# The up product of a feed-forward layer by seven half-size products of block sums, in two passes

## What is computed

```python
h = rmsnorm(x, g_ffn[i])
u = jnp.einsum("bsd,df->bsf", h, w_up[i])            # w_up: 1024 x 5632
f_gate = causal_dwconv(u[..., :D_FF], conv_f_w[i]) + conv_f_b[i]   # D_FF = 2816, 3 taps
f = jax.nn.gelu(f_gate, approximate=True) * u[..., D_FF:]
x = x + jnp.einsum("bsf,fd->bsd", f, w_down[i])      # w_down: 2816 x 1024
```

## Time and profile before

| | us |
|---|---|
| median of 3 runs | 2114.32 |
| lowest, highest | 2111.88, 2114.84 |
| profiled execution, time | 2106.84 |
| profiled execution, span | 2105.1 |
| PE busy in the span | 2044.3 |

### The profile page before, as it was taken

One profiled execution on the slowest core, in us unless ns is written; L12 is line 12 of the kernel. 1 busy time (PEld: TensorE's weight loads), 2 busy tenths in 40 slices (PEclk: granted clock), 3 DMA queues, 4 the chain that ended last, 5 costly groups with the idle time before them and its releaser, 6 DMA issues.

```text
span 2105.1 us, 24958 instructions
## 1 busy us (share of the span) xinstructions
PE 2044.3 (97%) x9797; PEld 1696.9 (81%) x9797; DVE 1177.0 (56%) x1119; ACT 439.1 (21%) x547; POOL 730.4 (35%) x534
## 2 busy tenths in 40 slices
PE   6999999999999999999999999999999999999998
PEld 5888788888887888888888888888788878888887
DVE  4999995312546755665565655745443745556520
ACT  4000001302222000000000000243222235555411
POOL 2444355444323343333333343423122511112221
PEclk9999999999999999999999999999999999999999
DMA  4211111241122122211222112211113210000033
GB/s 135 60 41 50 40 45 45 65 115 50 48 84 79 40 71 80 60 59 43 76 70 70 50 50 80 73 32 36 40 60 110 76 41 1 11 11 1 1 131 90
DMA packets 176852, 122.08 MB, mean 58 GB/s; under 512 B 8772, under 2 KB 160273, under 8 KB 176785
## 3 DMA queue, kind: packets, MB, share of 16 engines
q1 hardware_dynamic: 175504, 118.77, 18.7%
q10 hardware_dynamic: 1280, 2.35, 0.3%
HBM read 112.71 MB, written 8.39 MB: 58 GB/s over the span
## 4 chain that ended last, share of the span: by engine, by line
PE 79%; DVE 7%; issue 4%; POOL 4%; DMA 4%; ACT 3%; SPq 0%; POOLq 0%; DVEq 0%; ACTq 0%
PE ps L488 67%; POOL wlo L437 2%; DMA raw<-in_w_up 2%; PE ps L882 2%; POOL whi L435 1%; DVE prob L1878 1%; PE ps L896 1%; PE ps L893 1%; PE ps L899 1%; PE ps L915 1%; PE ps L890 1%; PE ps L917 1%; PE ps L916 1%; PE ps L902 1%; PE ps L705 1%
## 5 line engine op out<-in xcount | busy, mean ns | idle before, releaser
L437 POOL TENSOR_TENSOR wlo<-raw,whi 128x1024 fp32r<-128x1024 f32 (+2 forms) x162 | 459.1, 2834 | 13.5
L434 POOL TENSOR_TENSOR small<-ones 128x1 f32<-128x1 f32 x166 | 50.4, 304 | 1109.8 <-PE ps L488 916.3
L488 PE MATMUL ps<-xb_hi,whi 128*128 128x512 f32 x1216 | 378.6, 393 | 10.2 <-POOL wlo L437 3.5
L488 PE MATMUL ps<-xa_hi,whi 128*128 128x512 f32 x1184 | 372.5, 394 | 2.6 <-POOL wlo L437 1.1
L488 PE MATMUL ps<-xb_lo,whi 128*128 128x512 f32 x1216 | 375.0, 390 | 0.0
L488 PE MATMUL ps<-xb_hi,wlo 128*128 128x512 f32 x1216 | 374.5, 389 | 0.0
L488 PE MATMUL ps<-xa_lo,whi 128*128 128x512 f32 x1184 | 368.0, 390 | 0.0
L488 PE MATMUL ps<-xa_hi,wlo 128*128 128x512 f32 x1184 | 367.6, 389 | 0.0
L488 PEld LDWEIGHTS ps<-xb_hi,whi 128*128 128x128 f32 x1216 | 226.0, 188 | 64.1 <-POOL wlo L437 7.5
L488 PEld LDWEIGHTS ps<-xb_hi,wlo 128*128 128x128 f32 x1216 | 228.3, 188 | 48.1
L488 PEld LDWEIGHTS ps<-xb_lo,whi 128*128 128x128 f32 x1216 | 228.3, 188 | 48.1
(11 more groups left out here) (325 smaller groups left out, 2245.6 us busy)
## 6 DMA issues: line engine op xcount, KB each, us to landing
raw<-in_w_in SPq DMA_DIRECT2D x52, 512.0 KB, 3.8
raw<-in_w_up SPq DMA_DIRECT2D x44, 512.0 KB, 4.2
raw<-in_w_down SPq DMA_DIRECT2D x22, 512.0 KB, 3.5
w_mod<-in_w_mod SPq DMA_DIRECT2D x40, 256.0 KB, 2.9
x_columns<-in_x SPq DMA_DIRECT2D x8, 512.0 KB, 4.8
raw<-in_w_o SPq DMA_DIRECT2D x8, 512.0 KB, 3.8
raw<-in_w_ple_gate SPq DMA_DIRECT2D x8, 512.0 KB, 3.7
y_scratch<-resid SPq DMA_DIRECT2D x8, 512.0 KB, 3.1
```

The costliest lines, as they stand in the source:

```text
L434: nc.gpsimd.tensor_tensor(small[:, 106 + slab.slot:107 + slab.slot], ones[:, 0:1], ones[:, 0:1], ALU.mult)
L437: nc.gpsimd.tensor_tensor(lo, src, f32(hi), ALU.subtract).then_inc(split_done, 1)
L488: ins = mm(dst[j], w, r[j], start=first and f, stop=last and l)
```

## The change

The up product and the down product become two passes.

**Up pass.** The first two tiles (gate and up) are done as before, in four jobs. For each of the other 20 tiles the two weight tiles (gate, up) and the two halves of the 1024 input features form a 2 x 2 block matrix `A`, and the two halves of the features by the two halves of the tokens a 2 x 2 block matrix `B`. The product of the two is made from 7 products of blocks instead of 8 (Strassen's scheme in Winograd's form): four sums of weight blocks (`weight_sums`, on DVE, S1 to S4) and four sums of input blocks (`token_comb`, once, 128 x 2048 each), seven products (`combination`, 12 matmuls of 512 columns, each into its own PSUM bank), and seven additions that read PSUM (`comb_pair`). ACT makes the high part of each weight block (`weight_hi`) into a ring of four halves of `whi`, POOL the low part (`comb_split`). ACT also does the first tap and copies the first product out of PSUM. The input sums are built from `R` times `g_ffn` before the norm's factor is known. The finished f tile goes to a DRAM scratch (`f_store`). On DVE, ACT, POOL and SP the pairs run in hardware loops of two or four; the last four pairs are written out on DVE and ACT.

**Down pass.** Five chunks of four tiles and one of two. The f tiles come back from DRAM (`f_load`), ACT makes their high parts (`f_hi`), POOL the low parts (`f_low`, but for two that DVE makes). A down job has 24 matmuls (12 in the last chunk), a slab serves two jobs. The modulation's rows are now loaded by ACT's queue, four buffers deep, and accumulated behind the down jobs, on average 1.4 rows (two accumulations each) per job (`mod_rows_at`).

```diff
+        def combination(q, u, n):
...
+            if n == 0:
+                pe.wait_ge(sem("st_copied"), q * 4 + (u + 1))
+            else:
+                pe.wait_ge(sem("st_read"), q * 40 + (10 * u + (1, 3, 4, 6, 7, 9)[n - 1]))
+            pe.wait_ge(sem("st_split"), q * 28 + (g + 1))
...
+            for k in range(4):
+                w = slice(cols.start + k * P, cols.start + (k + 1) * P)
+                for i, (wp, bp) in enumerate(((whi, bh), (whi, bl), (wlo, bh))):
+                    last = mm(o, wp[:, s, w], bp[:, k, :], start=k == 0 and i == 0, stop=k == 3 and i == 2)
...
+        def comb_pair(q, u, following):
...
+            kept, summed = T[3][:, first], T[3][:, second]
+            P2 = product(1)
+            dve.wait_ge(sem("st_copied"), q * 4 + (u + 2))
+            step(tt(T[0][:, 2:2 + H], P2, kept, ALU.add))
+            after(1)
+            step(tt(T[0][:, 2:2 + H], T[0][:, 2:2 + H], rbc[:, first], ALU.mult))
+            step(tt(summed, product(2), kept, ALU.add))
+            P7 = product(3)
+            after(3)
+            step(tt(kept, P7, summed, ALU.add))
+            if following is not None:
+                weight_sums(*following)
+            P5 = product(4)
+            after(4)
+            dve.wait_ge(sem("f_ready"), t)
+            step(tt(T[2][:, second], P5, kept, ALU.add))
+            step(tt(summed, P5, summed, ALU.add))
+            P3 = product(5)
+            after(6)
+            step(tt(T[0][:, 2 + H:2 + S], P3, summed, ALU.add))
+            after(7)
+            step(tt(T[0][:, 2 + H:2 + S], T[0][:, 2 + H:2 + S], rbc[:, second], ALU.mult))
+            step(tt(T[2][:, first], product(6), kept, ALU.add))
+            after(9)
+            step(tt(T[2][:, 0:S], T[2][:, 0:S], rbc[:, :], ALU.mult))
+            taps(t)
+            after(10)
+            dve.wait_ge(sem("gelu"), t + 1)
+            tt(T[1][:, 0:S], T[1][:, 0:S], T[2][:, 0:S], ALU.mult).then_inc(sem("f_ready"), 1)
...
+        def comb_out(q, u, final=False):
...
+            fn(T[3][:, 0:H], PS[:, 0:H], ACT.Copy).then_inc(sem("st_copied"), 1)
+            weight_hi(q, g + 4)
+            weight_hi(q, g + 5)
+            gelu(q * 4 + (u + 1))
+            weight_hi(q, g + 6)
+            if not final:
+                for n in range(7, 10):
+                    weight_hi(q, g + n)
...
+            act.wait_ge(sem("st_read"), q * 40 + (10 + 10 * u + 8))
+            act.wait_ge(sem("f_out"), t * 16)
+            fn(T[1][:, 0:S], T[0][:, 0:S], ACT.Identity, scale=dcol("conv_f_w", t), bias=dcol("conv_f_b", t)).then_inc(sem("fc_tap"), 1)
+            if not final:
+                weight_hi(q, g + 10)
...
+        def mod_rows(rs):
...
+                if r >= 4:
+                    act.wait_ge(sem("mod_mac"), 2 * r - 5)
...
+        for c in range(NDC):
+            if 1 <= c:
+                rows_until(c - 1, 3)
+                f_hi(c, range(f_tiles(c)))
...
+                for c in range(NDC):
+                    for k in range(2 if c in (0, NDC - 1) else 4):
+                        split(L + (4 * c + k + (2 if c == 0 else 0)))
+                        if k == 1 and c < NDC - 1:
+                            f_low(c + 1)
```

More of the change, by code:

```diff
@@ L20 @@
 NF = DFF // P
-FC = 2
-NCH = NF // FC
+NDC = 6
+PAIRS = NF - 2
+MODG = 3 * D // H
 PLE = 256
@@ L336, in mod_rows @@
[L336 to L349, removed]
@@ new lines, in tensor_program @@
+        pe.wait_ge(pair_free[0], (Lin(JOBS["ffn"]) + 4).half())
+        with pe.Fori(0, PAIRS // 4) as q:
+            for u in range(4):
+                for n in range(7):
+                    combination(q, u, n)
+        J, L = Lin(JOBS["down0"]), Lin(SLABS["down"])
+        pe.wait_ge(pair_free[0], J.half())
+        pe.wait_ge(pair_free[1], J.half())
+        pe.wait_ge(split_done, L.val(1))
+        hi, lo = f_parts(0)
+        pe.wait_ge(sem("st_copied"), PAIRS + 1)
+        pe.wait_ge(sem("st_read"), 10 * PAIRS + 4)
@@ new lines, in tensor_program @@
+        for k in range(4):
+            if k < 2:
+                pe.wait_ge(sem("f_lo"), k + 1)
+            else:
+                pe.wait_ge(sem("tc_dve"), k + 5)
+            for m in range(2):
+                w = slice(k * 2 * P + m * P, k * 2 * P + m * P + P)
+                last = split_products([pair(J + m, 0, H), pair(J + m, H, S)], whi[:, 0, w], wlo[:, 0, w],
+                                      [hi[:, k, 0:H], hi[:, k, H:S]], [lo[:, k, 0:H], lo[:, k, H:S]], k == 0, k == 3,
+                                      1 if k == 0 and m == 0 else None)
+                if k == 3:
+                    last.then_inc(job_done, 1)
@@ L686, in tensor_program, with columns_due, hook @@
             transposes(Lin(JOBS["p"] + k), [pstage[:, t, k * P:(k + 1) * P] for t in range(8)])
[L687 to L699, removed]
+        def columns_due(c):
+            def hook(m):
+                of = 8 * c + m - 3
+                for g in range(MODG):
+                    if 8 * g + 7 in mod_rows_at(of // 8, of % 8):
+                        pe.wait_ge(sem("mod_read"), g + 1)
+                        mod_columns(g, 16 * (g + 1) + 1)
+            return hook
+        for c in range(1, NDC - 1):
+            ffn_down(c, between=columns_due(c))
         def square_sums(m):
@@ new lines, in vector_program @@
+        first_tap(1)
+        taps(1)
+        first_up(1)
+        dve.wait_ge(job_done, JOBS["ffn"] + 4)
+        weight_sums(0, 0)
+        first_product(1)
+        with dve.Fori(0, PAIRS // 4 - 1) as q:
+            for u in range(4):
+                comb_pair(q, u, (q, u + 1))
+        q = PAIRS // 4 - 1
+        for u in range(4):
+            comb_pair(q, u, (q, u + 1) if u < 3 else None)
+        for k in (2, 3):
+            dve.wait_ge(sem("f_hi"), k + 1)
+            tt(f_parts(0)[1][:, k, :], fraw[FSLOT[0]][:, k, :], f32(f_parts(0)[0][:, k, :]), ALU.subtract).then_inc(sem("tc_dve"), 1)
@@ new lines, in vector_program @@
+        dve.wait_ge(sem("cs"), 2)
+        for c in range(NDC - 1):
+            if c == 1:
+                for k in range(2):
+                    J = Lin(JOBS["p"] + k)
+                    dve.wait_ge(sem("pt_hi"), k + 1)
+                    tt(XAl[:, 4 + k, :], pair(J), f32(XAh[:, 4 + k, :]), ALU.subtract).then_inc(*one(free(J)))
+            for m in range(8):
+                down(c, m)
+                if mod_rows_at(c, m):
+                    for r in mod_rows_at(c, m):
+                        g, k = r // 8, r % 8
+                        if r == 0:
+                            dve.wait_ge(sem("f_out"), 16 * NF)
+                        if k == 4 and g:
+                            read_mod(g - 1)
+                        dve.wait_ge(sem(f"modw_in{r % 4}"), 16 * (r // 4 + 1))
+                        for n in range(2):
+                            mod_mac(k, n, mod_row_buffer(r), 16 * g + 1, g % 2)
```

526 lines of the change are left out of this document (353 added, 173 removed).

## The result

The changed kernel takes 2099.86 us (median of 4 runs, 2099.18 to 2101.82); the kernel before, timed beside it, 2113.1 (4 runs, 2111.12 to 2114.84). The ratio is 0.9939, with a 95% interval of 0.9922 to 0.9956: 0.6% faster, where I had forecast 1.2% slower. 2099.86 is within a microsecond of rival A. The span of the profiled execution is 2097.4 us, 7.7 less than before.

The account below looks back on a forecast made before the run. PE's matmul count was taken as the bound. Terms -54.4 - 8.4 + 44 + 8 + 32 + 5 gave +26: span 2131, median 2140.5 us, 1.2% slower; range 2098 to 2168.

Parts of the forecast that it names:

- rival A: Up loop: subtracts fall beside VectorE's PSUM reads and waits, cycle is PE's 19.04 us; 2100.5 us, chance 0.22.
- Term 1: Up product: twenty tile pairs take 84 matmuls instead of 96, 240 fewer in all; -54.4 us.
- Term 2: Old feed-forward loop: PE's waits for POOL's weight splits, five times 1.7 us, go with that loop; -8.4 us.
- Term 3: Up loop: VectorE's work, gaps and collisions with POOL's subtracts make a 21.8 us cycle per pair; +44 us, bounds 0 and 68.
- the old loop's 38%: Old feed-forward loop: VectorE's taps and accumulations lose 53 us of 140 us of POOL subtracts, at lower VectorE load.
- a layout: Up loop: one pair laid out by hand, VectorE losing 4.6 us, 50% of the 9.1 us of POOL subtracts.
- the point where the sign changed: Up loop: a cycle of 20.5 us, with 3.3 us of blocking instead of 4.6, divides slower from faster.
- Term 4: Before the up loop: the four token sums are covered by the first two tile pairs; cost 0, up to 5 us.
- Term 5: Passage from up to down: late first low parts, VectorE's residual add and the f load delay PE; +8 us, bounds 3 and 15.
- Term 6: Down pass, chunks 1 to 3: queue order delays the third slab's split, PE waits 7.4 + 13.0 + 11.3; +32 us.
- Term 7: Down pass and passage: PE's clock is slow after three long waits and the passage; +5 us, 0 to 12.
- Rival D: Up loop: seven banks in turn with PE waits lower the clock for a third of the loop; 2200 us, chance 0.03.

Follow-up runs that it names:

- the run with two extra sums: Changed kernel with the first weight sum computed two extra times in each up pair on VectorE: 2111.5 us.
- the run with three orders: Changed kernel with GpSimd's next-chunk low parts after the fourth split, VectorE's first weight sums before the taps, and its low parts 2 and 3 before the last product: 2062.3 us.
- two runs: Changed kernel with ScalarE issuing high parts after job 0's w_mod rows, 2065.9 us; or with GpSimd making low parts after the fourth slab's split, 2061.47 us.
- the runs with extra sums: Changed kernel with the first weight sum computed extra times per up pair: one 2103.2 us, two 2111.5, four 2145.8.

## Why the prediction was wrong

The direction was wrong, and one term of the sum decided it: VectorE's cycle in the up loop.

- **Term 1, matmuls, right.** -54.4 us: 1656 matmuls in 378.38 us, a cycle of 19.04.
- **Term 2, the loop's split waits**, -8.4: the split waits of the old loop are gone from the up loop. The trace of before lists only 3.5 us of them (7 waits between 690 and 1340); most of the rest of the 8.4 came from taking 0.2267 us for every matmul, where a stretch of whole jobs has 54.72 / 240 = 0.2280.
- **Term 3, VectorE in the up loop, +44, was 0: the step that failed.** Predicted cycle 21.8 us, own cycle by the runs 18.0. The 3.8 us are two errors. Work and gaps were 17.1 in the sum and are 18.0 - 3.3 = 14.7: I took one tap's idle time of 0.15 us for all 13 dependent steps, and took durations as if they added, where the trace has the next operation start 0.60 or 0.71 us after one of 0.69. That is 2.4 us. The blocking by GpSimd was 4.6 and is 3.3 in the run with two extra sums, 36% of the subtracts and not 50: near the old loop's 38%, which I had and overruled with a layout. That is 1.3. With the first alone mended the cycle would have been 19.4 and the sum about -12; with the second alone 20.5, the point where the sign changed. Both together put VectorE 1.0 us under PE, and the term at its lower bound.
- **Term 4, before the loop**, 0, was 3.3 us of wait and 2.8 of slow matmuls (13 in 5.72 us). The token sums do find cover; what failed is that I priced only them. The sums of the first pair's weights stood behind `taps(1)` and `first_up(1)`; with them ahead of `taps(1)`, in the run with three orders, the wait and the slow matmuls were gone.
- **Term 5, from up to down**, +8: waits of 1.4, 0.3, 4.6 and 0.5, 6.8 us. The size holds. Its second half doesn't: the residual add cost 0.5 and not 2.6 behind the squares of ctx. It became a wait of 4.2 only when the low parts were moved.
- **Term 6, the down pass, right.** 7.75 + 13.02 + 11.80 = 32.6 us against 7.4 + 13.0 + 11.3, by the chain laid out, and two runs took it away.
- **Term 7, the clock**, +5, was 7.6: six slow matmuls after the first wait, ten after each of the other two (1.3 + 2.1 + 2.1 us), and ten behind the 4.6 us wait (2.1). The windows behind the first two waits have a granted clock of 0.68 (1145 to 1150) and 0.54 (1205 to 1210). The Trainium skill (TensorE: Matmul & The Clock Gate, Loop structure matters more than you think) has PE go cold in long waits between matmuls; these rows agree, and also show that the loss isn't in proportion to the wait. Rival D did not occur: with seven banks in turn and no waits the granted clock between 700 and 1040 us is 1.00.

With term 2 as predicted, the terms add up to -54.4 - 8.4 + 0 + 6.1 + 6.8 + 32.6 + 7.6 = -9.7. The stretch to hold this against lies between two places that both kernels have: the 16 matmuls on `ones` and `rbc` early in the up product (626.53 us before, 625.91 after) and the four matmuls on `t` and `ones` behind the last down jobs (1394.56 and 1385.25). It is 8.7 us shorter; another 0.6 were gained ahead of it and 1.6 lost behind it, where nothing was changed, which makes the span's 7.7. That the sum comes so near is partly luck, since it leaves things out: with 3.5 us for term 2, the 4.9 us of other waits that the old kernel had between 628 and 690 us, and 3.5 us of small new waits that no term holds, it is -6.2. The 2.5 us between I can't assign. The medians fell by 13.2, since the profiled execution of before lies 6.3 us under its median and that of after on it.

Rival A had the outcome, VectorE keeps up, but not the mechanism. It let the subtracts fall beside PSUM reads and waits, and they didn't: the collisions still cost 3.3 us in a pair by the runs (3.8 in the changed kernel). VectorE keeps up for the larger part because its steps take 2.4 us less than I added up, which no rival named. So that A's 2100.5 hits the median is luck, in its reason and in its sum: its terms add to -14, 4 us below those above.

## What to carry to other kernels

Where one term decides the sign, don't build an engine's cycle from durations plus a gap read once: take start-to-start distances, for dependent and for independent neighbours, from a stretch where that engine is dense. An engine at 87% beside a bound one tells nothing of its room; adding a known operation once, twice and four times does. And look first for an instruction that waits in a queue ahead of work that is ready: here one number in one loop was worth 38 us, most of the 54.4 us that the saved matmuls bring.

## What the runs showed of the hardware

- Start-to-start distances on VectorE at 512 float32 columns (changed kernel, 833 to 842 us): 0.60 us for independent neighbours, 0.71 for dependent ones with a semaphore between, where one operation lasts 0.68.
- An operation of VectorE that collides with GpSimd waits for what is left of the subtract: the same product lasted 1.23 us with the subtract cut, 1.82 in the changed kernel and 2.36 in the runs with extra sums, by its place against GpSimd's. With the first tap on VectorE it lasted 1.23 beside whole subtracts.
- The clock can fall after PE has resumed. In the run with three orders (GpSimd's and VectorE's in two places) the matmuls at 1057.85 to 1059.34, after 3.5 us of waiting, have full pace, and those from 1059.34 to 1062.72 take 0.42 us each; then again from 1069.39, after 4.2 us.

```profile
1057.85 0.73 PE L607 MATMUL ps<-xa_hi,whi 128*128 128x512 f32 x2 [3.46 <-DVE xa_lo L1975]
1058.42 0.62 PE L607 MATMUL ps<-xa_lo,whi 128*128 128x512 f32 x2
1058.88 0.63 PE L607 MATMUL ps<-xa_hi,wlo 128*128 128x512 f32 x2
1059.34 1.02 PE L607 MATMUL ps<-xa_hi,whi 128*128 128x512 f32 x2
1060.16 1.05 PE L607 MATMUL ps<-xa_lo,whi 128*128 128x512 f32 x2
```
